# A bidirectional scan whose query-key products are kept for the other direction, with query norms taken from transposed tiles

## The chip, the cores and the metric

The kernel runs on one core of a Trainium2 chip. The metric is the device time of one execution in microseconds; smaller is better. Five engines work side by side and are tied by semaphores: TensorE (PE: matrix products and transposes into PSUM), VectorE (DVE), ScalarE (ACT), GpSimd (POOL) and SyncE (SP, which here only issues transfers). An engine works through its own instructions strictly in order, so an instruction that waits holds all those behind it.

## What is computed

One layer of a hybrid trunk on 1152 tokens (1024 latent ones and 128 context ones) of width 1024: a modulated norm, an input projection, a gated convolution group beside a bidirectional gated delta rule of 4 heads of width 128, an output projection, then a convolutional gated feed-forward part. The change is inside the delta rule only. Cut to what matters:

```python
def chunked_gated_delta(q, k, v, beta, log_alpha, s0):
    ...
    qk = jnp.einsum('bhnid,bhnjd->bhnij', q, k) * dec_incl
    ...
    def step(s, inp):
        u_c, w_c, qk_c, qd_c, ke_c, dl_c = inp
        v_new = u_c - jnp.einsum('bhcd,bhde->bhce', w_c, s)
        o_c = jnp.einsum('bhcd,bhde->bhce', qd_c, s) + jnp.einsum('bhij,bhje->bhie', qk_c, v_new)
        s = s * dl_c + jnp.einsum('bhcd,bhce->bhde', ke_c, v_new)
        return s, o_c
...
q = l2norm(q.reshape(b, l, DN_HEADS, DK)) * (DK ** -0.5)
...
o_f, s_f = chunked_gated_delta(q, k, v, beta[:, :, 0], log_alpha[:, :, 0], s0_f)
o_b, s_b = chunked_gated_delta(rev(q), rev(k), rev(v), ...)
o = o_f + rev(o_b)
```

The product of queries and keys of one tile of tokens is the same for both directions. Only the decay `dec_incl`, by which it is multiplied, differs.

## The kernel before, in words

The program first runs the input projection block by block, with the convolutions, the tables of decays and the inverses of the small triangular systems beside it. Then comes the scan, and then the output projection and the feed-forward part, where TensorE does products without a break.

The scan works on tiles of 128 tokens. `tile_of(d, x)` says which tile direction d (0 forward, 1 backward) treats at step x. Tiles 0 to 7 are the latent ones, and direction 1 takes them as 7, 6, ..., 0; step 8 is the context tile, number 8, for both. So each latent tile is treated twice: in steps 0 to 3 by one direction and in steps 4 to 7 by the other. Each engine has a hand-written order (`delta_pe`, `delta_act`, `delta_dve`, `delta_pool`), a loop over x from -1 to 8 that finishes step x (the scan part) and prepares step y = x + 1.

One round of TensorE, in order: `with_state(0)` (keys times state, then decayed queries times state), `first_products`, `with_state(1)`, `solve` for both directions, `closing` (from x = 6 on: transposes of finished outputs), `to_state(0)`, `second_products`, `queries(0)` (keys times queries of tile y), `to_state(1)`, `queries(1)`, `third_products`, `within(0)`, `query_rows`, `within(1)`, `fourth_products`. Each of the groups at line 1111 is four 128x128 products, one for each head. The first, second, third and fourth products build the inverse for the next tile from its blocks, with copies in between: M (DVE, L952), off-diagonal blocks (ACT, L736 and L740, in `off_blocks`, which also waits until DVE has written TX at L970, `low_diagonal`), LZ (DVE, L1025, `z_copy`) and the corner (ACT, L749). "First" to "fourth" below mean these products.

One round of VectorE: the wanted values (L908, `wanted`) of direction 0, M, the wanted values of direction 1, the diagonal (L960), `finish` (L941, from x = 6 on), `low_diagonal` (L970), new state 0 (L919), `values` (L979, twice), `weights(0)` (L985: keys-queries product from PSUM times decay R in SBUF), new state 1, `weights(1)`, `z_copy`, `second_out(0)` (L927, from x = 4 on), the copy of the query norms (L1030), `second_out(1)`, and from x = 5 on the sums of squares (L933, L935). POOL adds the mask to the decays R (L679, `masked`: both inputs in SBUF, when the transfer of the raw row has landed and `weights` has used the old R) and makes the decayed queries (L685, `decayed`, after an exponential on ACT, L812).

The squared norm of each query takes three steps: ACT squares the query tile (L820), TensorE multiplies the squares by a column of ones (L1171, `query_rows`, four products with one moving column), and DVE copies the four columns (L1030) to `ssq`, which only the output norm reads.

## Time and profile before

| | before |
|---|---|
| time, median of 3 runs | 1594.95 us (1590.67 to 1599.37) |
| the profiled execution | 1592.07 us, of which the span 1590.3 us |
| PE busy / DVE busy / ACT busy / POOL busy | 1530.6 / 942.6 / 476.4 / 398.4 us |
| chain that ended last | PE 86%, DVE 6%, DMA 3%, ACT 2%, issue 2% |
| the line with the scan's products (L1111) in that chain | 5% |
| TensorE clock granted over the span | 0.992 |

The median and the profiled execution are different executions of the same kernel. In the trace, times are counted from the start of the span. The scan lies between 466 and 621 us. A TensorE row "x8" of four products has eight records, since each of these float32 products is executed as two.

### The profile page before, as it was taken

The page shows a single profiled execution, that of the slowest core. Times are in us where ns is not written, and L with a number is a line of the kernel's source. Part 1 is how long each engine was busy: PE and PEld are TensorE (multiplying, and loading weights), DVE is VectorE, ACT ScalarE, POOL GpSimd, SP SyncE. Part 2 cuts the span into 40 slices and gives each one's busy share as a digit, 9 for nine tenths or more (in the row PEclk, how much of TensorE's full clock was granted, in tenths as well). Part 3 has the DMA queues.
Part 4 walks back from the last instruction along what each step waited for, and adds up shares of the span by engine and source line. Part 5 has one row for each costly group of instructions (what it writes and reads, how often), then busy time and mean ns, then how long its engine had stood idle before and what let it go on. Part 6 is the DMA issues. An engine that isn't in the chain of part 4 may idle for free.

```text
span 1590.3 us, 24156 instructions
## 1 busy us (share of the span) xinstructions
PE 1530.6 (96%) x9852; PEld 1474.9 (93%) x9852; DVE 942.6 (59%) x1407; ACT 476.4 (30%) x833; POOL 398.4 (25%) x204
## 2 busy tenths in 40 slices
PE   5899999999999998999999999999999999999997
PEld 1798999999989997998999999999999999999996
DVE  2752453569997795336885266528643673467257
ACT  4331254221166665125321032121212210221024
POOL 0011111560134343130231123113212321223120
PEclk9899999999999999999999999999999999999999
DMA  9543224532427446120111111111111111111103
GB/s 350 201 184 146 100 74 127 170 113 87 141 80 248 145 152 239 40 67 1 40 54 41 40 41 41 53 42 40 40 40 41 46 48 40 41 40 40 41 1 119
DMA packets 74641, 142.88 MB, mean 90 GB/s; under 512 B 19228, under 2 KB 44900, under 8 KB 72868
## 3 DMA queue, kind: packets, MB, share of 16 engines
q1 hardware_dynamic: 70932, 134.00, 25.0%
q10 hardware_dynamic: 3168, 5.51, 0.9%
q8 instruction: 87, 1.43, 0.4%
q0 software_dynamic: 432, 1.77, 0.3%
q14 instruction: 22, 0.18, 0.0%
HBM read 120.60 MB, written 20.65 MB: 89 GB/s over the span
## 4 chain that ended last, share of the span: by engine, by line
PE 86%; DVE 6%; DMA 3%; ACT 2%; issue 2%; SPq 1%; POOL 0%; DVEq 0%; ACTq 0%; POOLq 0%
PE ps L2312 49%; PE ps L2314 24%; PE ps L1111 5%; DMA araw<-wts 2%; PE ps L2253 1%; DVE ptmp L1922 1%; DVE lanes L1926 1%; PE ps L2263 1%; PE ps L2517 1%; DVE fa L2147 1%; PE ps L1084 1%; PE ps L2421 1%; DMA q<-q_d 0%; PE ps L2380 0%; PE ps L1056 0%
## 5 line engine op out<-in xcount | busy, mean ns | idle before, releaser
L2312 PE MATMUL ps<-hH,wH 128*128 128x384 f32 x1680 | 567.7, 338 | 7.3 <-DVE hL L1751 3.6
L2314 PE MATMUL ps<-hL,wH 128*128 128x384 f32 x1680 | 563.0, 335 | 0.0
L1225 POOL TENSOR_TENSOR wL<-raw,wH 128x1024 fp32r<-128x1024 f32 x93 | 226.2, 2432 | 887.3 <-ACT wH L1423 886.8
L2312 PE MATMUL ps<-hH,wL 128*128 128x384 f32 x1680 | 382.4, 335 | 0.0
L2312 PEld LDWEIGHTS ps<-hH,wH 128*128 128x128 f32 x1680 | 316.6, 188 | 15.2 <-issue 12.6
L1423 ACT ACTIVATE wH<-raw 128x1024 fp32r<-128x1024 f32 x99 | 105.1, 1062 | 710.4 <-PE ps L2312 709.4
L2314 PEld LDWEIGHTS ps<-hL,wH 128*128 128x128 f32 x1680 | 316.7, 189 | 0.0
L2147 DVE SCALAR_TENSOR_TENSOR fa<-G,cst,fa 128x1024 f32<-128x1024 f32 x176 | 295.5, 1679 | 15.4 <-DVE fa L2147 0.6
L2312 PEld LDWEIGHTS ps<-hH,wL 128*128 128x128 f32 x1680 | 300.2, 188 | 0.0
L2312 PE MATMUL ps<-pH,wH 128*128 128x384 f32 x528 | 179.2, 339 | 4.1 <-DVE pL L2171 1.8
L2034 DVE SCALAR_TENSOR_TENSOR X<-ps,mod,X 128x384 f32<-128x384 f32 x138 | 70.5, 567 | 188.9 <-PE ps L2312 188.9
L2314 PE MATMUL ps<-pL,wH 128*128 128x384 f32 x528 | 177.1, 335 | 0.0
L2312 PE MATMUL ps<-pH,wL 128*128 128x384 f32 x528 | 123.1, 336 | 0.0
L2143 DVE TENSOR_SCALAR fa<-G,cst 128x1024 f32<-128x1024 f32 x22 | 16.6, 753 | 164.3 <-ACT G L1439 164.3
L2312 PEld LDWEIGHTS ps<-pH,wH 128*128 128x128 f32 x528 | 99.7, 189 | 7.0 <-DVE X L2036 3.2
L2314 PEld LDWEIGHTS ps<-pL,wH 128*128 128x128 f32 x528 | 99.6, 189 | 0.7
L2312 PEld LDWEIGHTS ps<-pH,wL 128*128 128x128 f32 x528 | 94.8, 189 | 0.0
L1783 DVE TENSOR_SCALAR acc<-zp,wqk 128x1024 f32<-128x1024 f32 (+1 forms) x24 | 21.8, 946 | 72.7 <-ACT zp L1439 72.7
L1284 POOL TENSOR_TENSOR pL<-fa,pH 128x1152 fp32r<-128x1152 f32 x16 | 53.8, 3366 | 23.6 <-ACT pH L1645 23.6
L2253 PE MATMUL ps<-araw,scT 128*32 128x512 f32 x192 | 37.6, 686 | 18.5 <-DMA araw<-wts 18.3
L2253 PEld LDWEIGHTS ps<-araw,scT 128*32 128x32 f32 x192 | 6.2, 115 | 41.7 <-DMA araw<-wts 29.6
L2164 DVE TENSOR_TENSOR fa<-fa,ps 128x384 f32<-128x384 f32 x66 | 32.6, 548 | 11.8 <-PE ps L2312 11.8
(316 smaller groups left out, 1869.0 us busy)
## 6 DMA issues: line engine op xcount, KB each, us to landing
raw<-wts SPq DMA_DIRECT2D x103, 512.0 KB, 3.3
araw<-wts SPq DMA_DIRECT2D x48, 512.0 KB, 6.1
X<-xT SPq DMA_DIRECT2D x8, 1152.0 KB, 13.7
kv<-tok_d SPq DMA_DIRECT2D x16, 512.0 KB, 4.9
tok_d<-stage ACTq DMA_DIRECT2D x18, 256.0 KB, 2.0
q<-q_d SPq DMA_DIRECT2D x18, 256.0 KB, 5.8
gb<-grow_d SPq DMA_DIRECT2D x18, 256.0 KB, 3.6
y<-X SPq DMA_DIRECT2D x8, 384.0 KB, 2.4
```

Of the source, the lines that this page charges most:

```text
L1111: last = M(ps[:, k, h * P:h * P + P], left(h), right(h), start=(start if start is not None else h == 0), stop=(stop if stop is not None el ...
L1225: nc.gpsimd.tensor_tensor(weight(1, u4), raw[:, u4 % RAW, :], weight(0, u4).bitcast(F32), ALU.subtract).then_inc(s["wl_ready"], 1)
L1284: nc.gpsimd.tensor_tensor(pL[:, slot, :], fa[:, f % 2, :], pH[:, slot, :].bitcast(F32), ALU.subtract).then_inc(s["pL_ready"], 1)
L1423: A(weight(0, u4), raw[:, u4 % RAW, :], ACT.Copy).then_inc(s["wh_ready"], 1)
L1783: last = V.tensor_scalar(dst, src, w(tap), None, ALU.mult)
L2034: last = V.scalar_tensor_tensor(xs(lo, hi), bank3(side, n)[:, 0:hi - lo], mod[:, gate * 8 + ob, 0:1], xs(lo, hi), ALU.mult, ALU.add)
L2143: V.tensor_scalar(dst, src, w(3 * dy + dx), None, ALU.mult)
L2147: last = V.scalar_tensor_tensor(dst, src, w(3 * dy + dx), dst, ALU.mult, ALU.add)
L2164: last = V.tensor_tensor(fa[:, f4 % 2, n * TW:n * TW + TW], fa[:, f4 % 2, n * TW:n * TW + TW], bank3(side, n), ALU.mult)
L2253: last = M(ps[o:o + Q, ada_bank(m), :], scT[:, kt, :], araw[:, a % ARAW, 512 * j:512 * j + 512], start=(kt < 2), stop=(kt >= KT - 2))
L2312: last = M(out, lhs, rh[:, c], start=(k == 0 and not lo), stop=(lo and k == kts - 1))
L2314: M(out, lhs, rl[:, c], start=False, stop=False)
```

## The change

- `queries` (keys times queries) is done for steps 0 to 3 in both directions, and once in step 8. ACT copies each of the eight products of steps 0 to 3 from PSUM to SBUF tiles `KQ` (`keep`), after `weights` has used it. In steps 4 to 7 `weights` multiplies the kept tile instead of one in PSUM, so that both its inputs are in SBUF.
- In step 8 both directions use one product, and it is computed after the third products.
- Query norms: TensorE transposes the query tile (`query_rows`), ACT squares the transposed tile out of PSUM, and DVE sums the squares along each row (`query_sums`, 128x512 to 128x4). Those of step 0 are made in the round x = 0, after `with_state(0, 0)` and the first products.
- `low_diagonal` now stands ahead of `finish` on DVE.
- The loads of `ycA` (two of 1152 KB), whose place the kept tiles take until then, go from round y = 1 to y = 7 and y = 8; the load of the query tile of direction 0 waits for the transposes in place of the squares.

```diff
+    KQ = [place(f"KQ{k}", [P, H, P], F32, blk(14 - k // 4 * 2) + k % 4 * H * P * 4) for k in range(8)]
...
+    HALF = LAST // 2
+    def kept(d, y):
+        return KQ[2 * (LAST - 1 - y if y >= HALF else y) + (1 - d if y >= HALF else d)]
...
                     b, t = dl[d], tile_of(d, y)
-                    seen(sp, "qk", d, y)
+                    seen(sp, "qk", d, min(y, HALF))
                     seen(sp, "q_decayed", d, y)
                     if d == 0:
-                        sp.wait_ge(s["q_sq"], y)
+                        sp.wait_ge(s["trq"], y)
...
         def query_squares(act, y):
-            landed_at(act, "q_in", 0, y + 1)
+            act.wait_ge(s["trq"], y + 1)
             if y:
-                act.wait_ge(s["trq"], y)
+                act.wait_ge(s["q_sum"], y)
+            else:
                 act.wait_ge(s["solved"], 3)
-            nc.scalar.activation(qsq_of(y), q_of(0, y)[:], ACT.Square).then_inc(s["q_sq"], 1)
+            nc.scalar.activation(qsq, heads(bank_of(0)[3]), ACT.Square).then_inc(s["q_sq"], 1)
...
+            def keep(d, y):
+                seen(act, "pt", d, y + 1)
+                A(kept(d, y)[:], heads(bank_of(d)[3]), ACT.Copy).then_inc(s["kept"], 1)
...
                         new_values(d, x)
+                if x == 0:
+                    query_squares(act, 0)
...
+                if y < HALF:
+                    keep(0, y)
+                if 0 <= x < LAST // 2:
+                    first_out(0, x)
                 if 0 < y < TT_:
                     query_squares(act, y)
-                if 0 <= x < LAST // 2:
-                    first_out(0, x)
+                if y < HALF:
+                    keep(1, y)
...
             def weights(d, y):
                 b = dl[d]
-                seen(dve, "qk", d, y + 1)
                 seen(dve, "r_exp", d, y + 1)
-                done(V.tensor_tensor(b["PT"][y % 2][:], heads(bank_of(d)[3]), R_of(d, y), ALU.mult), "pt")
+                if y < HALF:
+                    seen(dve, "qk", d, y + 1)
+                    src = heads(bank_of(d)[3])
+                elif y < LAST:
+                    dve.wait_ge(s["kept"], 2 * HALF)
+                    src = kept(d, y)[:]
+                else:
+                    dve.wait_ge(s["qk"], 2 * HALF + 1)
+                    src = heads(bank_of(0)[3])
+                done(V.tensor_tensor(b["PT"][y % 2][:], src, R_of(d, y), ALU.mult), "pt")
+            def query_sums(y):
+                dve.wait_ge(s["q_sq"], y + 1)
+                V.tensor_reduce(ssq[:, tile_of(0, y), :], qsq, mybir.AxisListType.X, ALU.add).then_inc(s["q_sum"], 1)
...
+                if pre and y:
+                    low_diagonal(y)
                 for d, t, i in closed(x):
                     finish(d, t, i, bank_of(d)[3])
-                if pre and y:
-                    low_diagonal(y)
+                if x == 0:
+                    query_sums(0)
...
             def query_rows(y):
-                seen(pe, "pt", 0, y + 1)
-                pe.wait_ge(s["q_sq"], y + 1)
-                for h in range(H):
-                    last = M(ps[:, bank_of(0)[3], h:h + 1], qsq_of(y)[:, h, :], mat("ones")[:, 0:1], start=True, stop=True)
-                last.then_inc(s["trq"], 1)
+                seen(pe, "pt", 0 if y < LAST else 1, y + 1)
+                if y < HALF:
+                    pe.wait_ge(s["kept"], 2 * y + 1)
+                if y >= HALF:
+                    pe.wait_ge(s["q_sq"], y)
+                    seen(pe, "o_final", 0, max(y - 6, 0))
+                    landed_at(pe, "q_in", 0, y + 1)
+                turn(bank_of(0)[3], lambda h: q_of(0, y)[:, h, :]).then_inc(s["trq"], 1)
...
                 if x == 0:
+                    query_rows(0)
...
-                if pre:
+                if y < HALF:
                     queries(0, x, y)
                 if scan:
                     to_state(1, x)
-                if pre:
+                if y < HALF:
                     queries(1, x, y)
                 if pre and y:
                     third_products(pe, y)
+                if y == LAST:
+                    queries(0, x, y)
                 if scan:
                     within(0, x)
-                if pre:
+                if pre and y:
                     query_rows(y)
```

## Rows read from the trace of the kernel before

**Rows 1.** Busy by stretch: length, each engine, PE clock, DMA share, GB/s.

```profile
548.40:564.90 16.50, 16.50 (x219) 15.75 (x217) 13.85 (x32) 9.81 (x30) 7.76 (x7) 1.00 0.45 137
564.90:584.70 19.80, 19.80 (x248) 19.05 (x248) 18.58 (x36) 13.76 (x38) 13.14 (x10) 1.00 0.39 118
```

**Rows 2.** Chain that ended last, late in round x = 4: start, us, what.

```profile
548.42 2.88 PE ps L1111 x24
551.29 1.07 PE ps L1084 x16
...
553.46 0.79 PE ps L1171 x8
...
598.45 0.88 PE ps L1106 x8
```

**Rows 3.** Timeline of DVE, round x = 4: start, us, line, operation, [idle before].

```profile
543.78 1.13 DVE L908 SCALAR_TENSOR_TENSOR Y<-ps,SC,vb 128x128 f32<-128x128 f32 x4 [0.24 <-PE ps L1111]
...
551.37 0.68 DVE L985 TENSOR_TENSOR PTb<-ps,R 128x512 f32<-128x512 f32 x1
...
553.00 0.68 DVE L985 TENSOR_TENSOR PTb<-ps,R 128x512 f32<-128x512 f32 x1
553.60 0.73 DVE L1025 TENSOR_SCALAR LZ<-ps 64x256 f32<-64x256 f32 x2
...
557.26 1.13 DVE L908 SCALAR_TENSOR_TENSOR Y<-ps,SC,vb 128x128 f32<-128x128 f32 x4 [1.29 <-PE ps L1111]
```

**Rows 4.** Timeline of PE, same round and the next: fourth products' end, next round.

```profile
555.17 0.50 PE L1096 MATMUL ps<-LZ,TX 64*64 64x64 f32 x5
556.06 1.16 PE L1111 MATMUL ps<-S,QKV 128*128 128x128 f32 x8
```

**Rows 5.** Timeline of ACT, round x = 4.

```profile
550.42 0.27 ACT L740 ACTIVATE TX<-ps 32x128 f32<-32x128 f32 x1
...
551.90 0.61 ACT L820 ACTIVATE ptmp<-q 128x512 f32<-128x512 f32 x1
```

**Rows 6.** Timeline of POOL and DVE, round x = 4: where the two overlap.

```profile
549.06 1.84 POOL L685 TENSOR_TENSOR qd<-gb,q 128x512 f32<-128x512 f32 x1
549.68 1.76 DVE L979 TENSOR_TENSOR vb<-kv,SC 128x512 f32<-128x512 f32 x1
552.68 1.28 POOL L679 TENSOR_TENSOR R<-gb,cst 128x512 f32<-128x512 f32 x1 [1.78 <-DMA gb<-grow_d]
```

**Rows 7.** Lines: durations min/median/max of one, first and last start.

```profile
L979 DVE TENSOR_TENSOR vb<-kv,SC x16: 678/686/1777, 482.2 to 603.3; 128x512 f32<-128x512 f32 x16
```

**Rows 8.** Timeline of DVE and POOL, end of scan: a sum beside POOL's work.

```profile
616.20 0.69 DVE L933 TENSOR_REDUCE red<-osq 128x4 f32<-128x512 f32 x1 [5.56 <-POOL osq L693]
616.12 1.04 POOL L693 TENSOR_TENSOR osq<-oTok 128x512 f32<-128x512 f32 x1
```

**Rows 9.** Timelines of PE, ACT and POOL, start of the scan.

```profile
470.75 1.05 PE L1171 MATMUL ps<-cst,qd 128*128 128x1 f32 x8 [2.53 <-DVE PT L985]
471.60 1.04 ACT L1423 ACTIVATE wH<-raw 128x1024 fp32r<-128x1024 f32 x1
476.80 1.28 POOL L679 TENSOR_TENSOR R<-gb,cst 128x512 f32<-128x512 f32 x1 [0.72 <-DMA gb<-grow_d]
479.29 1.05 ACT L853 ACTIVATE Y<-ps 128x512 f32<-128x512 f32 x2
```

**Rows 10.** Timelines of DVE, PE and ACT, rounds x = 6 and 7.

```profile
583.63 1.46 DVE L970 TENSOR_TENSOR TX<-XT,cst 64x256 f32<-64x256 f32 x1
586.78 0.67 PE L1084 MATMUL ps<-TT,LZ 64*64 64x64 f32 x8 [1.70 <-ACT TX L740]
593.12 1.13 DVE L908 SCALAR_TENSOR_TENSOR Y<-ps,SC,vb 128x128 f32<-128x128 f32 x4
604.30 0.67 PE L1084 MATMUL ps<-TT,LZ 64*64 64x64 f32 x8 [1.10 <-ACT TX L740]
608.96 0.78 ACT L749 ACTIVATE TT<-ps 64x256 f32<-64x256 f32 x2 [2.89 <-PE ps L1096]
```

More of the change, by code:

```diff
@@ L637, in _ @@
                         og_load(d, tile_of(d, 4), 0)
[L638 to L639 removed]
+                if y in (HALF + 3, HALF + 4):
+                    k = y - HALF - 3
+                    seen(sp, "pt", 1, (HALF + 2, LAST)[k])
+                    sp.dma_start(ycA[:, 2 * k:2 * k + 2, :].bitcast(F32), yc_d[:, 4 * k:4 * k + 2, :].bitcast(F32)).then_inc(s["ycA_in"], 16)
             after_split(ahead - 1, U_OUT + 1 + RAW, 0)
```

24 lines of the change are left out of this document (10 added, 14 removed).

## Prediction

> **What bounds the kernel now.** I read in this order: the busy share by stretch, the chain that ended last, then each engine's timeline of one round. Outside the scan nothing changes, so only the stretch 466 to 621 us counts. By stretch, a middle round is 16.50 us long and PE is busy in all of it, DVE in 13.85 us; the round x = 6 with its neighbourhood shows DVE at 18.58 of 19.80 us [rows 1]. The chain says the same: in round x = 4 it stays on PE, three groups of four 128x128 products in 2.88 us, then the third products, then `query_rows` in 0.79 us [rows 2]. So a reader would take 0.96 us off for each group removed. But a busy PE only says that PE is the last of several engines that are nearly level. How far behind the others are is what their timelines show.
>
> DVE works from the wanted values of direction 1 at 543.78 without a gap to LZ, ending at 554.33 [rows 3]. The fourth products, which need LZ, start on PE at 555.17, and the next round at 556.06 [rows 4]. So PE can come forward by at most 0.77 us (keeping the 0.07 us that a handover takes) before it waits for DVE. On ACT the last off-diagonal block ends at 550.69 [rows 5], and the third products, which need it, start at 551.29 in the chain [rows 2]: 0.5 us of room. ACT and DVE both hang on products early in the same round, not on the ones removed. TensorE's clock is granted in full in these rounds (1.00) [rows 1], so it can gain nothing there.
>
> **The change part by part.** The sum is made against the profiled execution, 1592.07 us (span 1590.3); the median of the runs, 1594.95, is 2.9 above it, and I add that at the end.
>
> *Products dropped.* Eight groups in steps 4 to 7 and one in step 8, 9 x 0.96 = 8.6 us of PE [rows 2]. In rounds x = 3 to 5 PE then reaches the third products at 549.4 in place of 551.3 on the clock of round 4, and stands until ACT is done at 550.7. From there the order is third, `within(0)`, `query_rows`, `within(1)`, and then it waits for LZ. Of 1.9 us a round, 0.5 goes to the wait for ACT, or 0.77 at most comes through by DVE's limit.
>
> *The product from SBUF.* `weights` reads kept tile and decay, both in SBUF. A DVE operation of 128x512 with two SBUF inputs takes 686 ns undisturbed and 1777 when POOL is in its way [rows 7]; from PSUM the product took 680 [rows 3]. What the second figure is: `values` starts at 549.68 while POOL multiplies queries (549.06 to 550.90), and ends at 551.44, 0.54 behind POOL's end [rows 6]. `weights(0)` at 551.37 finds POOL idle. `weights(1)` at 553.00 falls into POOL's `masked(0)`, 552.68 to 553.96 [rows 3, 6]. Held in the same way it ends at 553.96 + 0.54 = 554.50 in place of 553.68: +0.82 us. LZ then ends at 555.15; the fourth products of direction 0 can start behind its first half and those of direction 1 behind its second, and the next round starts near 555.72 in place of 556.06. So -0.34 us a round, not -0.77. The bounds are the two: -0.77 (never held) and +0.9 (PE fully behind a product that waits for a whole mask). I take -0.34, by the row it repeats. The Trainium skill ("SBUF — State Buffer", section "Who interferes with whom") has the rule: a VectorE instruction with two SBUF inputs and a GpSimd instruction that reads SBUF exclude each other for the whole instruction, and one with a single SBUF input is free. By that rule, the product held before was free and is not now; the trace agrees in the 1777 ns row. The skill's "VectorE: DVE Perf Modes", in its section on the TRN2 errata, speaks for the change: a fixed 58 cycles with an SBUF source against 120 from PSUM, an estimate of 65 ns a product and 0.5 us for eight; the trace (686 against 680 ns) doesn't show it, and the sum leaves it out.
>
> *Query norms.* Transposes of a tile took 0.88 us (L1106) against 0.79 for the products with one column [rows 2]: +0.09 in each of the nine rounds; on the path only in x = 0 to 2, +0.27, since in the others PE waits anyway. ACT squares as before, 0.61 us [rows 5], but later, between `query_rows` and the corner, where it has room. DVE's copy of four columns becomes a sum over 128x512, 0.69 us, not held by POOL (it ran beside POOL's square) [rows 8]: +0.54 a round, behind LZ. Its cover is DVE's gap before the next wanted values, 1.29 us in round 4 [rows 3]. From x = 5 on the sums of squares fill that gap: at 593.12 the wanted values start with no idle time before them [rows 10]. There it counts.
>
> *Copies kept.* Eight on ACT, 0.6 us each (its copies and squares of 128x512) [rows 5], in rounds x = -1 to 2. The first of a round starts when `weights(0)` ends, 0.6 us before `query_rows` needs it. Behind them on ACT stand the square, the corner and the exponentials of the next round, and ACT is busy in 9.81 of the 16.50 us of a round [rows 1]: 0, and if that cover is gone 0.6 each.
>
> *Start.* PE had waited 2.53 us for the first product before `query_rows(0)` [rows 9]; with the state products ahead of it that wait is filled. But behind the move `with_state(1)` waits for the first copy, and ACT makes it after the weights' half at 471.60 to 472.64, so near 473.3; transposes to 474.2; and the next stage waits anyway: ACT's new values at 479.29 come behind exponentials that wait for POOL's mask at 476.80, which waits for a transfer [rows 9]. 0, with -0.3 and +0.5 as bounds (SP's query load, now behind the transposes, had been issued about when they end).
>
> *Loads moved.* SP's queue: `ycA`, in round y = 1, competed for transfers; in y = 8 it stands ahead of the gate tiles of the next `finish` and ahead of `ycB`, needed after 621 us; in the round of x = 6 the transfer engines are busy for 0.39 of the time [rows 1]. 0; 1 at the bound if that cover is gone.
>
> *Late rounds.* x = 5: DVE's end of round comes 0.54 + 0.78 later, and its gaps before the next M and wanted values take that up, so nothing of PE's gain is left: 0. x = 6: `low_diagonal` ahead of `finish` releases ACT's blocks, for which PE stood 1.70 us [rows 10], but at that place it meets POOL's squares and then its query products; I take 0.6 us earlier (bounds 0 and 1.9). Then sum, held product and `finish`, now behind it, put the next wanted values +0.65. x = 7: the last product stands behind the third products. From their start to the fourth it was 3.9 us; now it is third 1.07, product 0.96, the two `weights` from it 1.35, transposes 0.9, `within(1)` 1.0 = 5.3, and the third start 0.2 later than at 604.30. So the corner on ACT, 608.96 before [rows 10], comes +1.45 us later (including x = 6), and table loads, norms and the last step all hang on it.
>
> Sum: start 0, x = 0 to 2 +0.27, x = 3 and 4 2 x -0.34 = -0.68, x = 5 0, x = 6 and 7 +1.45: **+1.0 us**, 1593.1 on the profiled execution, 1596.0 on the median. 8.6 us of TensorE work go into waits.
>
> **Rivals.** (a) *PE's time comes through in full*: -8.6 + 0.8 for transposes = -7.8, 1584.3 own, 1587.2 median. For it: PE is busy in every row. Against: DVE's unbroken chain to LZ. (b) *The product is not held, and `low_diagonal` gets its turn*: -0.77 in x = 3 and 4, about 1 us less in x = 6 and 7: -1.0, 1591.1 own, 1594.0 median. (c) *Slower: both products are held.* If POOL's second query product ends more than 0.47 us later than 550.90, it covers the start of `weights(0)` too, and masks follow; each of rounds 3 to 6 then costs a further mask, 1.27 us: +1.0 + 5.1 = 1598.2 own, 1601.1 median. (d) *The copies on ACT reach the path* in x = -1 to 2 (they do not hide): 8 x 0.6 = +4.8, 1597.9 own, 1600.8 median.
>
> **How the numbers follow.** Forecast 0.70, (b) 0.13, (a) 0.04, (c) 0.08, (d) 0.05. The time is the forecast's, 1596.0. The three runs of before spread by 4.4 us to either side of their median, and the median of the changed kernel will miss its own level by some 2 or 3; forecast and (b) with that reach from 1589 to 1600, and 1601 takes in part of (c) and (d). Within 0.5% (8 us, about what a measurement here can tell from no change) lie all cases, (a) only just: faster 0.03, same 0.94, slower 0.03.
>
> **What would show it.** Rounds x = 3 to 5 of about 16.2 us with PE idle before the third products (waiting for ACT's TX) and before the fourth (waiting for DVE's LZ); PE busy some 8 us less in a scan of the same length; one of two `weights` a round near 1.5 us beside `masked`; `low_diagonal` in x = 6 ending near 584.5; the corner of x = 7 later against its round. Wrong if rounds x = 3 to 5 are near 14.6 us (then LZ doesn't bound), if the held product stays at 0.69, or if rounds 0 to 2 grow by over 0.3 us.

## The result, and the profile after

The changed kernel takes 1610.38 us (median of 4 runs, 1609.22 to 1612.67) beside 1594.49 for the kernel before in the same comparison (4 runs, 1590.67 to 1599.37). The ratio is 1.010 with a 95% interval of 1.0069 to 1.013: slower by 1%. I had forecast 1596.0 and a range of 1589 to 1601. In the later comparisons, of 24 to 28 runs each, the median of the kernel before is 1596.8 to 1598.9 us with single runs from 1588.8 to 1604.4; every ratio below is to the kernel before in the same comparison, and every trace is one execution.

| | before | after |
|---|---|---|
| the profiled execution / its span | 1592.07 / 1590.3 us | 1609.58 / 1607.8 us |
| first query-key product starts | 466.3 | 465.2 |
| from there to the next stage's first product (the scan) | 155.0 | 161.1 |
| of it, up to the first product of round x = 1 (the start) | 23.8 | 26.8 |
| of it, each of the rounds x = 1, 2 / 3 / 4, 5 | 16.49 / 16.50 / 16.49 | 16.04 / 15.95 / 17.12 |
| of it, rounds x = 6 / 7 with the last step | 19.06 / 29.61 | 19.27 / 32.76 |
| from there to the end | 969.0 | 981.5 |
| TensorE clock granted over the span | 0.992 | 0.982 |

So the 17.5 us between the two profiled executions are +6.1 in the scan, -1.1 ahead of it, and +12.5 behind it, where the change touches no computation. But the +6.1 is the difference of two single executions. The traces of pad24, pad224, bpad32 and bmatch (below) hold the same two scans once more each, as they only have more wait instructions at the start of the program (us):

| trace | start | x = 1, 2 | x = 3 to 5 | x = 6, 7 | scan |
|---|---|---|---|---|---|
| code of before: before | 23.8 | 33.0 | 49.5 | 48.7 | 155.0 |
| bpad32 | 24.6 | 33.0 | 49.5 | 53.4 | 160.4 |
| bmatch | 24.6 | 33.0 | 49.5 | 53.3 | 160.3 |
| changed code: after | 26.8 | 32.1 | 50.2 | 52.0 | 161.1 |
| pad24 | 23.3 | 32.1 | 50.4 | 52.0 | 157.8 |
| pad224 | 23.1 | 32.1 | 52.0 | 53.0 | 160.1 |

What repeats is -0.9 us in x = 1 and 2 and +0.7 to +2.5 in x = 3 to 5. The start and the two late rounds differ as much between traces of one code as between the codes. By the means, 158.6 and 159.7, the scan is 1 us longer, and the loss is what lies behind it.

Lines of the changed kernel: L1143 is the helper that was L1111, L1116 the third products, L1138 the transposes, L1011 `weights`, L997 `values`, L746 ACT's TX, L2351 and L2353 the later stages' products.

The busy share by stretch of the changed kernel, rounds x = 4, 5, 6 and x = 7 with the last step:

```profile
core 0: us, PE busy (x) PEld busy (x) DVE busy (x) ACT busy (x) POOL busy (x), PEclk, DMA share, GB/s
539.99:557.11 17.12, 15.90 (x198) 15.03 (x197) 14.84 (x31) 9.82 (x30) 6.68 (x6) 0.90 0.50 157
557.11:574.23 17.12, 15.89 (x199) 15.03 (x197) 14.88 (x32) 9.87 (x30) 7.26 (x6) 0.90 0.44 131
574.23:593.50 19.27, 16.71 (x207) 15.50 (x205) 18.66 (x37) 13.12 (x36) 10.94 (x8) 0.91 0.59 193
593.50:626.26 32.76, 24.53 (x254) 22.79 (x253) 22.57 (x43) 21.58 (x51) 12.02 (x11) 0.90 0.74 258
```

Against [rows 1], 20 records of PE are gone in a round and the round is longer, because PEclk is 0.90 where it was 1.00: in 0.2 of each round TensorE ran at 1.2 GHz in place of 2.4. The timeline of PE in round x = 4 shows where:

```profile
548.77 1.16 PE L1143 MATMUL ps<-Y,ke 128*128 128x128 f32 x8
551.15 0.71 PE L1116 MATMUL ps<-TT,LZ 64*64 64x64 f32 x8 [1.22 <-ACT TX L746]
551.66 1.06 PE L1116 MATMUL ps<-TX,LZ 64*64 64x64 f32 x8
552.65 2.07 PE L1143 MATMUL ps<-Y,PT 128*128 128x128 f32 x8
554.52 0.87 PE L1138 MATMUL ps<-cst,q 128*128 128x128 f32 x4
```

PE stands 1.22 us for ACT's TX, as the prediction said it would, and then a group of four products takes 2.07 us in place of 1.16. DVE in the same round:

```profile
551.75 0.68 DVE L1011 TENSOR_TENSOR PTb<-KQ,R 128x512 f32<-128x512 f32 x1
553.38 1.44 DVE L1011 TENSOR_TENSOR PTb<-KQ,R 128x512 f32<-128x512 f32 x1
554.75 0.74 DVE L1058 TENSOR_SCALAR LZ<-ps 64x256 f32<-64x256 f32 x2
```

One of the two `weights` is held to 1.44 us where it was 0.68 [rows 3]. Behind the scan, the timeline of PE at the head of the feed-forward loop, and the row of the waits view for 626 to 1607 us (in total, times, longest):

```profile
919.52 0.44 PE L2351 MATMUL ps<-hH,wH 128*128 128x384 f32 x1 [0.91 <-issue]
...
920.15 0.33 PE L2353 MATMUL ps<-hL,wH 128*128 128x384 f32 x1
922.57 0.33 PE L2351 MATMUL ps<-hH,wH 128*128 128x384 f32 x1 [2.08 <-issue]
```

```profile
PE ps L2351 <- issue: 10.6, 8, 2.1
```

At each of the four passes from the loop's end back to its head PE stands 1.8 to 2.1 us, a few products behind the head, and 0.5 to 0.9 us just ahead of them, and waits for nothing that the profile shows. Before, the same four places have one gap of 0.44 to 0.50 us:

```profile
1065.21 0.44 PE L2312 MATMUL ps<-hH,wH 128*128 128x384 f32 x1 [0.44 <-issue]
```

### The profile page after: what moved, and what is told of

It is laid out like the page before. It is cut to its first block, busy times and chain, and to the rows that moved or that the text cites. A ratio compares the mean times of both kernels' runs of the same rounds, so it can differ in the third digit from the quotient of the medians.

```text
span 1607.8 us, 23941 instructions
## 1 busy us (share of the span) xinstructions
PE 1534.0 (95%) x9744; PEld 1477.2 (92%) x9744; DVE 949.7 (59%) x1407; ACT 480.2 (30%) x841; POOL 403.7 (25%) x204
## 4 chain that ended last, share of the span: by engine, by line
PE 88%; DVE 5%; ACT 3%; DMA 2%; issue 2%; POOL 0%; DVEq 0%; ACTq 0%; SPq 0%; POOLq 0%
PE ps L2351 51%; PE ps L2353 25%; PE ps L1143 4%; DMA araw<-wts 2%; PE ps L2292 2%; DVE TT L978 1%; PE ps L2302 1%; PE ps L2556 1%; PE ps L1116 1%; DVE fa L2186 1%; PE ps L1088 1%; PE ps L2460 0%; PE ps L2419 0%; PE ps L1138 0%; DVE X L2073 0%
## 5 line engine op out<-in xcount | busy, mean ns | idle before, releaser
L2351 PE MATMUL ps<-hH,wH 128*128 128x384 f32 x1680 | 569.7, 339 | 16.1 <-issue 10.6
L2353 PE MATMUL ps<-hL,wH 128*128 128x384 f32 x1680 | 564.8, 336 | 0.0
L2351 PE MATMUL ps<-hH,wL 128*128 128x384 f32 x1680 | 384.3, 336 | 0.0
L2351 PEld LDWEIGHTS ps<-hH,wH 128*128 128x128 f32 x1680 | 318.0, 189 | 16.1 <-issue 13.3
L2353 PEld LDWEIGHTS ps<-hL,wH 128*128 128x128 f32 x1680 | 318.2, 189 | 8.7 <-issue 8.7
L2186 DVE SCALAR_TENSOR_TENSOR fa<-G,cst,fa 128x1024 f32<-128x1024 f32 x176 | 300.9, 1710 | 15.4 <-DVE fa L2183 0.6
L2351 PEld LDWEIGHTS ps<-hH,wL 128*128 128x128 f32 x1680 | 301.8, 189 | 0.0
L2351 PE MATMUL ps<-pH,wH 128*128 128x384 f32 x528 | 179.4, 340 | 4.0 <-DVE pL L2210 1.8
L2353 PE MATMUL ps<-pL,wH 128*128 128x384 f32 x528 | 177.2, 336 | 0.0
L2351 PE MATMUL ps<-pH,wL 128*128 128x384 f32 x528 | 122.9, 335 | 0.0
L2351 PEld LDWEIGHTS ps<-pH,wH 128*128 128x128 f32 x528 | 99.6, 189 | 7.0 <-DVE X L2075 3.2
L2353 PEld LDWEIGHTS ps<-pL,wH 128*128 128x128 f32 x528 | 99.7, 189 | 0.7
L2351 PEld LDWEIGHTS ps<-pH,wL 128*128 128x128 f32 x528 | 94.8, 189 | 0.0
L1325 POOL TENSOR_TENSOR pL<-fa,pH 128x1152 fp32r<-128x1152 f32 x16 | 58.4, 3648 | 8.6 <-ACT pH L1684 8.6
```

The source lines that it names most:

```text
L1325: nc.gpsimd.tensor_tensor(pL[:, slot, :], fa[:, f % 2, :], pH[:, slot, :].bitcast(F32), ALU.subtract).then_inc(s["pL_ready"], 1)
L2186: last = V.scalar_tensor_tensor(dst, src, w(3 * dy + dx), dst, ALU.mult, ALU.add)
L2351: last = M(out, lhs, rh[:, c], start=(k == 0 and not lo), stop=(lo and k == kts - 1))
L2353: M(out, lhs, rl[:, c], start=False, stop=False)
```

## The experiments

The theory after the first look had two parts. L (loop): the change took 224 instructions out of PE's stream ahead of the feed-forward loop (by my count of the program), and the place of the loop's head in the stream decides what the jump costs. C (clock): with the products gone PE waits once more in a round, and TensorE's clock falls. The rival of L is that something else behind the scan changed (transfers, buffers); the rival of C is that the waits or the held product alone lengthen the rounds.

**pad24, pad224 and bpad32: the place of the loop's head.** All stand at the head of PE's program. Twice as many waits as instructions are written, as two go into one: 49 in pad24, 449 in pad224, and in the kernel before 65 for bpad32.

```diff
-            pe.wait_ge(s["sc_ready"], 2)
+            for _ in range(49):
+                pe.wait_ge(s["sc_ready"], 2)
```

> The changed kernel with 24 more instructions in TensorE's stream ahead of its first product (48 waits on a semaphore that already has its value, two to an instruction); nothing else. In the changed kernel TensorE stands about 2.1 us eleven instructions behind the head of its feed-forward loop, in four of five passes, with no engine that it waits for. Theory L (where the loop's head lies in the instruction stream decides whether the fetch behind the jump is late, and the change moved it by some 220 instructions): the head moves past that place, the four stalls go, and with them the half-clock stretches behind them at 922 and 1075 us: 8 us from the stalls and 2 to 5 us from the clock, so 1598 to 1601 us. Rival D (the stall comes from data, memory traffic or the engines beside it): 1610, stalls as before.

Measured: 1594.77 us (1591.35 to 1595.89; ratio to before 0.9978, interval 0.9959 to 0.9996). No gap at the loop's head; 966.5 us behind the scan (981.5), and the rounds x = 1 to 5 as in the changed kernel. 24 instructions more, 15.6 us less, and below the 1598 to 1601 that I expected. The half-clock stretch at 780 us, behind a wait for ACT, is there as in the changed kernel (at 782.5), so it is not the loop's.

> The changed kernel with 224 instructions more ahead of TensorE's first product, which puts the head of the feed-forward loop back to where it is in the kernel before (the change took 216 product and load instructions and 8 waits out). Theory L: no stall behind the loop's head, 1598 to 1601 us, the same as with 24. Rival D: 1610. If the scan alone made the whole loss, both stay at 1610.

Measured: 1609.54 us, ratio 1.007 (1.0049 to 1.0091): the expected time was missed, the mechanism not. The loop's gaps are 0.43 to 0.98 us and the part behind the scan takes 968.3 us as before. But PE's first product starts at 28.5 us in place of 5.1: the 224 waits themselves cost 0.10 us each, and the first query-key product comes 14 us late.

> The kernel before with 32 instructions more ahead of TensorE's first product. If the fetch works in blocks of 64, 128 or 256 instructions, the loop's head then lies against the blocks as in the changed kernel (224 less is 32 more). Theory L: the kernel before gets the four stalls of 2.1 us and some clock behind them, 1602 to 1607 us. Rival D: 1594, no stalls.

Measured: 1610.98 us, ratio 1.0085 (1.0058 to 1.0112), above the 1602 to 1607 expected. The kernel before, its computation unaltered, is as slow as the changed one, and shows the same gaps:

```profile
1075.89 0.44 PE L2313 MATMUL ps<-hH,wH 128*128 128x384 f32 x1 [0.96 <-issue]
...
1078.92 0.34 PE L2313 MATMUL ps<-hH,wH 128*128 128x384 f32 x1 [2.06 <-issue]
```

That excludes the rival of L: nothing that the change does to transfers or buffers is in this kernel.

The passes also show how gaps and clock share the loss. One pass, from a row that stands in each to its next, for example

```profile
868.43 0.44 PE L2351 MATMUL ps<-pH,wH 128*128 128x384 f32 x1 [0.32 <-DVE X L2075]
```

```profile
1023.79 0.45 PE L2351 MATMUL ps<-pH,wH 128*128 128x384 f32 x1 [0.32 <-DVE X L2075]
```

| | four passes, us | half the clock for 3.4 us in |
|---|---|---|
| before | 151.15, 151.07, 151.10, 151.11 | none |
| after | 155.36, 154.86, 153.19, 153.47 | the first (923.7) and second (1077.3) |
| bpad32 | 155.40, 153.81, 153.69, 153.66 | the first (923.7) |
| pad24 | 150.36, 150.36, 150.35, 150.36 | none |

The four passes hold 12.45 us of the +12.5. A pass with the gaps alone takes 153.2 to 153.8 us, one with a half-clock stretch behind them 1.1 to 2.2 us more.

**fill: an unused product in PE's wait.** In x = 3 to 5, four products of 128x128 (keys by the identity) into bank 3 of direction 1, which nobody reads then.

```diff
+                if HALF <= y < LAST - 1:
+                    idle_products()
                 if pre and y:
                     third_products(pe, y)
```

> The changed kernel with four products of 128x128 whose result nobody reads, in rounds x = 3, 4 and 5, where TensorE waits for the off-diagonal blocks; they go to PSUM bank 3, which is idle there (48 instructions more, so the loop's head moves too). In the changed kernel rounds 4 and 5 take 17.1 us, with the clock at half for 3.4 us in each. Theory C (the idle time ahead of the third products lets the clock fall, and that makes these rounds longer than before): the clock stays at 1.00 in rounds 3 to 5 and they take 15.9 to 16.1 us, 2.2 us less in the scan. Rival W (the waits for ScalarE and VectorE alone make them long, the clock is no matter): 17.1 us with the filler too. By theory L the feed-forward stalls are gone as well: in all 1595 to 1599 us; by D and C 1608.

Measured: 1589.26 us, ratio 0.9964 (0.9939 to 0.9989), below the 1595 to 1599 expected, with rounds of 16.2 to 16.3 us where I had expected 15.9 to 16.1. Round x = 5 by stretch, and PE in round x = 4:

```profile
552.43:568.66 16.23, 15.33 (x207) 14.44 (x205) 15.08 (x32) 9.88 (x30) 7.70 (x7) 1.00 0.47 140
```

```profile
547.25 0.68 PE L1116 MATMUL ps<-TT,LZ 64*64 64x64 f32 x8 [0.33 <-ACT TX L746]
...
549.32 0.60 PE L1138 MATMUL ps<-cst,q 128*128 128x128 f32 x4
...
551.50 0.50 PE L1128 MATMUL ps<-LZ,TX 64*64 64x64 f32 x5 [0.69 <-DVE LZ L1058]
```

Work that nobody uses makes the round 0.8 us shorter than with an idle PE. This isn't one trace's luck. after, pad24, pad224 and free0, with PE idle there, all fall to half the clock in x = 4 and 5 (17.1 to 18.7 us a round), and late3, free3, best3, own, own7 and own8, with the unused product, never do in x = 3 to 5 (15.5 to 16.1). And now the wait for LZ that I had forecast shows, 0.69 us: with the clock at half PE had been too late to meet it.

**free3 and free0: the held product, with and without the unused products.**

```diff
         def masked(pool, d, y):
-            seen(pool, "pt", d, y)
+            for k in range(2):
+                seen(pool, "pt", k, y)
```

> The kernel with unused products in rounds x = 3 to 5 (fill), and besides both of POOL's masks of a round wait until both weights products of DVE are done, so that weights(1), now with two SBUF inputs, cannot be held by masked(0). Nothing is left out. Theory 'weights(1) is held by the mask and its 0.7 us bounds the round' (the prediction's term +0.82 minus 0.77): weights(1) takes 0.69 us instead of 1.4, LZ and the fourth products come 0.7 us sooner, rounds x = 3 to 5 take 15.6 us instead of 16.28, the masks start 0.7 us later at no cost; time 2 us under fill. Rival 'the masks are wanted as soon': exponentials on ACT wait for them, the next round's new values slip by what was won, rounds stay at 16.3 and the time is that of fill.

Measured: 1589.35 us, ratio 0.9964 (0.9943 to 0.9986). The rounds went as expected, the time did not: x = 3, 4, 5 take 15.55, 15.54, 15.54 us, and the second `weights` in the round x = 4, which ends at 556.07, is

```profile
553.92 0.68 DVE L1012 TENSOR_TENSOR PTb<-KQ,R 128x512 f32<-128x512 f32 x1
```

The 2.2 us less in these three rounds don't show in the medians (1589.26 and 1589.35), whose single runs spread by 5 us and more. In free0 the masks are as in free3, without the unused products and with 48 wait instructions' worth at the start, so that the loop's head stands where it does in fill.

> The changed kernel with POOL's masks behind both weights products, without unused products; 48 waits' instructions in PE's waits of the first 25 us, so its loop head stands where that of fill and free3 does. Nothing is left out. With the changed kernel (hold, no filler: rounds x = 4, 5 of 17.12 us), fill (hold, filler: 16.3) and free3 (no hold, filler: 15.54) it completes the square. Theory 'hold and clock are two causes that add': weights(1) in 0.69 us, PE stands 1.2 us ahead of the third products, the clock falls to half for 3.4 us a round in x = 3 to 5 or 4 and 5, these rounds take 16.3 us; time 2 us above free3. Rival 'without the hold PE stands only once a round and keeps its clock': rounds of 15.2 to 15.5, time at or under free3's 1589.

Measured: 1593.3 us, ratio 0.9973 (0.9955 to 0.999). The square of the two causes, from seven traces (rounds x = 3, 4, 5 in us):

| | PE idle in the wait | unused product in it |
|---|---|---|
| `weights(1)` held | after 15.95, 17.12, 17.12; pad24 16.16, 17.10, 17.10; pad224 16.20, 18.63, 17.13 | fill 16.27, 16.34, 16.22; late3 15.95, 15.98, 16.08 |
| not held | free0 15.55, 17.11, 18.65 | free3 15.55, 15.54, 15.54 |

```profile
540.07:557.19 17.12, 15.89 (x199) 15.02 (x197) 14.20 (x31) 9.87 (x30) 7.25 (x6) 0.90 0.53 163
557.19:575.84 18.65, 17.44 (x198) 16.47 (x197) 15.27 (x33) 9.85 (x30) 7.35 (x6) 0.82 0.49 148
```

I had expected 16.3 us for the two causes apart. They are two causes, but they don't add: with the clock at half, taking the hold away brings nothing in x = 4 and 5, since PE is then the last again.

**norms3 and norms48: the change's one half alone.** The kernel before, with the norms of tiles 1 to 8 from transposed tiles, and every product computed twice. norms48 has 145 more wait instructions in PE's waits of the first 50 us.

```diff
-                for h in range(H):
-                    last = M(ps[:, bank_of(0)[3], h:h + 1], qsq_of(y)[:, h, :], mat("ones")[:, 0:1], ...)
+                turn(bank_of(0)[3], lambda h: q_of(0, y)[:, h, :]).then_inc(s["trq"], 1)    # y > 0
```

> The kernel before with one half of the change: for tiles y = 1 to 8 the query norms come from transposed tiles squared on ACT and summed on DVE; tile 0 as before, all query-key products computed twice as before, low_diagonal and the loads as before. Its loop head lies 65 instructions before that of the kernel before, 159 behind that of the changed kernel, so by the position theory no 2-us stalls. Theory by the records of the changed kernel (a tile's transposes are 4 records in 0.6 us, not 8 in 0.88 as I had read): PE is on the path of rounds x = 1 to 5 and each takes 16.0 to 16.1 us instead of 16.5, without a wait of PE over 0.5 us and with the clock granted in full; late rounds +0.5 each for the sums; the scan 1 to 2 us shorter than before and the time about 1594 beside a before of 1596. Rival 'as I had priced it': rounds 16.6, scan 1 us longer, 1598.

Measured: 1594.58 us, ratio 0.9979 (0.9964 to 0.9995). Rounds x = 2 to 5 of 16.03 or 16.04 us with PE busy in all of it:

```profile
537.36:553.40 16.04, 16.04 (x215) 15.29 (x213) 13.76 (x31) 9.87 (x30) 5.50 (x5) 1.00 0.47 142
```

> The kernel norms3 (only the norms changed, every product computed twice) with 145 more wait instructions on PE in its waits of the first 50 us, so that its loop head stands where that of bmatch does, 304 behind the changed kernel's (48 past a multiple of 256). Nothing is left out. Theory 'position': no gaps at the loop's head (0.44 to 0.86 us in norms3), 965.5 us from the next stage's first product to the end (970.0 in norms3, 965.9 in bmatch), rounds x = 1 to 5 of 16.03 to 16.05 us with the clock in full, as in norms3; time 3 to 4 us under norms3's 1594.6 unless the added waits reach past PE's own waits (then the first query-key product comes later than 470 and the gain is eaten up). Rival 'norms3 was slow after the scan for another reason': 970 us again.

Measured: 1592.68 us, ratio 0.996 (0.9946 to 0.9975). No gaps at the head, 966.0 us behind the scan (970.0 in norms3). Beside bmatch (below), whose head stands at the same place and whose ratio is 1.0007, this half of the change makes the kernel faster, by some 0.4%.

**bmatch: the kernel before with its head at the good place.** 80 more wait instructions, in three of PE's own waits in the first 25 us.

> The kernel before with 80 more wait instructions on PE in its waits of the first 25 us (about 80 ns each, in gaps of 2.1, 2.1 and 5.2 us), so that its loop head stands 304 instructions behind that of the changed kernel, which is 48 behind a place where it stalls if the pattern repeats every 256 instructions, the place of fill. Nothing is left out. In the kernel before, 224 behind, PE stands 0.44 to 0.5 us at four of five passes of the loop, and from the next stage's first product to the end it takes 969.1 us; in fill, late3 and free3 (48 behind) no such gap and 964.5 to 966.1 us. Theory 'position, with a period of 256 instructions': no gaps over 0.4 us at the loop's head, 965 us from that product to the end, the scan as before (131 us from x = 1), time 3 to 5 us under the kernel before of the same runs. Rival 'the gaps and the 4 us come from the kernels' other parts': gaps of 0.44 us, 969 us, same time as the kernel before.

Measured: 1596.69 us, ratio 1.0007 (0.9991 to 1.0022). No gaps, 966.0 us behind the scan: the place is confirmed. The time is not: it is that of before, where I had expected 3 to 5 us less, and why is open. Its profiled execution shows a scan of 160.3 us with code that took 155.0 in the profile of before; 3.2 of the 5.4 us are in round x = 6, 1.5 in x = 7:

```profile
572.18:594.42 22.24, 20.54 (x226) 19.57 (x225) 18.99 (x40) 13.24 (x36) 10.72 (x8) 0.84 0.49 153
```

bpad32 has the same round (22.15 us). So the clock falls in x = 6 of the kernel before too, in two of three executions, behind the same wait of 1.70 us [rows 10], and the rows of before happened to show one where it didn't.

The place of the head over all traces, as instructions behind that of the changed kernel:

| head | kernels | gaps at the four passes, us | behind the scan, us |
|---|---|---|---|
| 0, 256 | after, bpad32 | 1.83 to 2.36 each, and 0.54 to 1.00 ahead of it | 981.5, 981.0 |
| 24, 48 | pad24, fill, late3, free3, free0, own, own7, own8 | none over 0.4 | 964.5 to 966.5 |
| 304 | bmatch, norms48 | none over 0.4 | 966.0, 966.0 |
| 72, 113, 120, 159, 224 | kept, best3, keptfill, norms3, before, pad224 | up to 0.4 to 1.0 | 968.3 to 970.1 |

It repeats with 256 instructions (0 with 256, 48 with 304); the differences of 1.5 us within the second row go with half-clock stretches of 3.4 us, which fill and free3 (964.5) lack at the start of this part. The Trainium skill ("Runtime: NRT & Kernel Launch", section "Instruction fetch mechanics") states that instructions come in blocks of 256 and that a taken branch breaks the sequential prefetch; the period in the traces agrees, with 1.8 to 2.4 us a jump at the worst place. That PE waits for a fetch there no row shows; the rows say only that it waits for nothing else.

**kept and keptfill: the other half.** kept is the changed kernel with the norms of the kernel before; keptfill adds the unused products of fill. Its start is not that of the changed kernel: the first `query_rows` is at its old place and must now wait for a copy on ACT (below).

> The other half of the change alone: query-key products kept for the other direction and not computed twice, low_diagonal ahead of finish and the loads as in the changed kernel, but the query norms as in the kernel before (squares of the queries on ACT, four products with one column, DVE's copy of four columns; tile 0 at its old place). Loop head 72 instructions behind that of the changed kernel, so no 2-us stalls. Nothing is left out. Theory 'the dropped products are what costs': rounds x = 1, 2 of 16.5 us as before, PE stands about 1 us ahead of the third products in x = 3 to 5, the clock falls to half there, these rounds take 17.1 us (16.5 before); from the first query-key product to the next stage 158 us (155.0 before, 154.9 with the norms alone); time 1 to 2 us above the kernel before less what the position gives back, 1595. Rival 'the norms' sums behind LZ are what costs': rounds x = 3 to 5 of 16.2 us, scan as short as before or shorter, 1590.

Measured: 1611.17 us, ratio 1.0098 (1.0061 to 1.0134), with no 2-us gaps at the loop. Right in kind for the clock, far off in size (1595 expected): it was at half for 17.1, 10.2 and 13.7 us, from 555.5, 579.4 and 599.9 (the expectations of this part give such times some 2 us too early). Rounds x = 4, 5, 6:

```profile
544.00:563.71 19.71, 18.49 (x203) 17.47 (x201) 14.45 (x31) 9.98 (x30) 7.41 (x7) 0.79 0.56 171
563.71:586.74 23.03, 21.82 (x202) 20.71 (x201) 15.70 (x34) 9.78 (x29) 5.88 (x5) 0.65 0.33 100
586.74:608.75 22.01, 20.96 (x210) 19.94 (x209) 17.59 (x39) 13.14 (x35) 10.36 (x8) 0.73 0.46 150
```

> The kernel kept (products kept for the other direction, old norms) with four unused products ahead of the third products in x = 3 to 5, as in fill. In kept TensorE had half its clock for 17.1, 10.2 and 13.7 us from 553, 577 and 598, and rounds x = 3 to 5 took 19.7, 23.0 and 22.0 us; the time was 1611.2. Loop head 48 instructions behind that of kept, gaps of 0.5 to 1 us there as in kept. Nothing is left out. Theory 'the dropped products cost through the clock alone': no half-clock stretch in x = 3 to 5, these rounds take 16.3 to 16.6 us, from the first query-key product to the next stage 157 us (174.9 in kept), time about 1595. Rival 'the kept half costs by its waits or copies': the rounds stay above 18 us and the time above 1605.

(The expectation's "x = 3 to 5" for these three rounds is off by one: they are x = 4 to 6.) Measured: 1603.26 us, ratio 1.0024 (1.0006 to 1.0041), 8 us less by adding work:

```profile
546.98:563.10 16.12, 15.77 (x211) 14.88 (x209) 13.84 (x31) 9.80 (x30) 5.17 (x5) 1.00 0.46 141
563.10:579.09 15.99, 15.66 (x210) 14.84 (x208) 14.32 (x33) 9.74 (x30) 7.41 (x7) 1.00 0.46 139
579.09:600.91 21.82, 19.58 (x211) 18.55 (x209) 19.89 (x41) 13.24 (x36) 11.89 (x9) 0.80 0.65 215
```

Where the unused products stand (x = 4, 5) the clock is full and 10.6 us are gone; x = 6, without them, is as long as in kept. The scan is 11 us shorter (163.9 for 174.9) but not the 157 expected, and both theories hold in part. The start took 29.0 us in kept and 28.6 in keptfill (23.8 before), since the first `query_rows` stood for the copy of the first product, which ACT makes only behind its work on the next stage's weights (471.37 to 472.41):

```profile
472.31 1.05 ACT L863 ACTIVATE KQ<-ps 128x512 f32<-128x512 f32 x2
```

```profile
472.98 1.84 PE L1209 MATMUL ps<-cst,qd 128*128 128x1 f32 x8 [5.03 <-issue]
```

So in the rounds this half costs through the clock, and at the start through a copy: the prediction's rival (d), in a place that the whole change avoids.

**late3, best3, own, own7, own8: the late rounds.** late3 is fill with the last product ahead of the third products; best3 adds unused products in x = 0, 6 and 7; own is free3 with the last product ahead of the third and `finish` ahead of `low_diagonal` for the last tile; own7 fills x = 7 by a bank that doesn't wait for `finish`; own8 besides moves a load:

```diff
-                if y in (HALF + 3, HALF + 4):
-                    k = y - HALF - 3
...
-            after_split(ahead - 1, U_OUT + 1 + RAW, 0)
+                if y == HALF + 3:
+                    ycA_load(0)
             for d in range(2):
                 og_load(d, tile_of(d, 5), 1)
+            ycA_load(1)
+            after_split(ahead - 1, U_OUT + 1 + RAW, 0)
```

> The kernel with unused products in rounds x = 3 to 5 (fill), and besides the last query-key product (x = 7) ahead of the third products instead of behind them. Nothing is left out; one product group changes its place, no instruction is added. In fill PE stood 3.37 us ahead of the third products of x = 7 (till 600.17), the product ran 602.04 to 604.1 at half the clock, DVE stood 3.29 us for it, and the corner on ACT started 607.75, 20.3 us behind the round's first product (17.3 in the kernel before). Theory 'the late round is long because the last product stands behind the third products' (the prediction's step): the product runs near 599.1 when finish of direction 0 is done, inside the wait; the two weights follow values without a gap (near 600.9), the corner comes 2 to 3 us sooner against its round (17.3 to 18.3 us), next stage 31 us behind the round's start instead of 33.4, time about 1587. Rival 'DVE's and POOL's new order (low_diagonal held by POOL, finish behind it) makes the round long': corner at most 0.5 us sooner, time 1589.

Measured: 1589.85 us, ratio 0.995 (0.9931 to 0.9969), x = 7 to the next stage 32.88 us (33.46 in fill), which is within what this stretch spreads by between traces. The theory fell: the product still ran only at 602.42, behind a wait of 2.53 us for DVE's `finish`, and the third products behind it.

> The changed kernel with unused products in all long waits of PE in the scan: ahead of the third products in rounds x = 3 to 7 (16 instructions each), and two groups at x = 0 ahead of query_rows(0), where PE stood 2.2 us for the first copy; the last query-key product ahead of the third products as in late. Loop head 113 instructions behind the changed kernel's. Nothing is left out. Theory 'clock and last product together explain the scan': no half-clock stretch between 466 and 621, x = 7 to the next stage 30 us, the scan 5 us shorter than in fill, no loop stalls, time about 1584, 0.8% under the kernel before. Rival 'the waits of x = 0, 6 and 7 are not where the clock is lost, or the unused products lengthen the round': time that of late, 1587, or above.

Measured: 1596.31 us, ratio 0.9989 (0.997 to 1.0009). A miss: its clock still fell at 478.6 and 601.5, as the unused products of x = 6 and 7 themselves waited for `finish` (3.07 us in x = 7), and its head stood at 113.

> The changed kernel with three things together, nothing left out: unused products in the wait of rounds x = 3 to 5 (as fill), POOL's masks behind both weights products (as free3), and in the last tile's round (x = 7) the last query-key product ahead of the third products (as late3) with finish ahead of low_diagonal, in the order of the kernel before. Loop head 48 instructions behind the changed kernel's. In late3 the product still stood 2.53 us for finish, which stood behind low_diagonal (held by POOL's squares), and ran at 602.42. Theory 'the late round is long because the last product hangs on finish, which the change put behind low_diagonal': the product runs within 0.5 us of the end of DVE's finish and before ACT's TX, PE's third products follow TX at once, x = 7 to the next stage 30 us (33.5 in fill, 32.9 in late3, 29.6 in the kernel before), rounds x = 3 to 5 15.5 us, from the first query-key product to the next stage 150.5 us (before 155.0, free3 153.0), time about 1586. Rival 'TX then comes later by what finish takes (1.4 us)': x = 7 stays at 32 us or more and the time is that of free3, 1589.

Measured: 1591.58 us, ratio 0.9951 (0.9934 to 0.9968); x = 7 took 34.64 us, longer than in late3. The rows of DVE and SP say why:

```profile
600.72 1.57 DVE L960 SCALAR_TENSOR_TENSOR oTok<-ps,onw,og 128x512 f32<-128x512 f32 x2 [2.34 <-DMA og<-gd]
```

```profile
589.53 0.65 SPq L645 DMA_DIRECT2D ycA<-yc  x1
590.23 0.42 SPq L493 DMA_DIRECT2D raw<-wts  x1
590.70 12.14 SPq L608 DMA_DIRECT2D og<-gd  x4
```

> As own, but three unused products (12 instructions) in place of four in rounds x = 3 to 5, and three more in x = 7 ahead of the last query-key product, into a bank that is free there, so that they don't wait for finish. In own PE stood 2.38 and 1.32 us in x = 7, TensorE had half its clock for 10.2 us from 598.2, and x = 7 to the next stage took 34.6 us. Nothing is left out. Theory 'the clock is most of what x = 7 loses': half for 3.4 us or less there, x = 7 to the next stage 32 us; rounds x = 3 to 5 15.2 to 15.5 us; time 2 us under own's 1591.6. Rival 'the gate tiles' transfer is all of it': x = 7 stays at 34 us, time that of own.

Measured: 1588.46 us, ratio 0.9943 (0.9925 to 0.9961); x = 7 33.74 us with `finish` still waiting 1.46 us, half the clock for 6.8 us from 597.0. Between the two theories.

> As own7, and besides the second ycA load (and the weights' load behind it) stand behind the gate tiles of the next finish in SP's queue, not ahead of them. In own DVE's finish of x = 7 stood 2.34 us for the gate tiles (issued 590.7, landed near 600.7) behind ycA (issued 589.5, 1152 KB); in the kernel before ycA had been loaded in x = 0. Nothing is left out. Theory 'the moved load holds the gate tiles' (my bound of 1 us in the prediction): finish follows diagonal with no wait (near 598.4 on own's clock), product, TX, third products 2 us sooner, x = 7 to the next stage 30 us, the time 2 us under own7, near 1587. Rival 'the tiles land no sooner, the transfer engines being full': finish still waits over 1.5 us, time that of own7.

Measured: 1586.45 us (4 runs, 1582.83 to 1588.66), ratio 0.9915 (0.9882 to 0.9947). `finish` follows with no wait, half the clock for 3.4 us from 603.4, x = 7 in 31.50 us (x = 6 and 7 together 49.5, 52.5 in own7):

```profile
597.62 1.40 DVE L963 SCALAR_TENSOR_TENSOR oTok<-ps,onw,og 128x512 f32<-128x512 f32 x2
```

```profile
588.63 1.35 SPq L608 DMA_DIRECT2D og<-gd  x2
590.03 2.93 SPq L612 DMA_DIRECT2D ycA<-yc  x1
```

This version beats both kernels, by 0.85% (interval 0.5 to 1.2%) and, across comparisons, 1.5%. Most of the second figure is the place of the loop's head: pad24, which is the changed kernel with its head at a good place, took 1594.77 us, 0.5% more than own8.

## Why the prediction was wrong, and where it was right

**The step that failed worst: "Outside the scan nothing changes".** +12.5 of the +17.5 us lie there, by the place of the loop's head; pad24 takes 15.0 of the 981.5 us away, bpad32 puts 12 onto the kernel before. The gaps themselves are 8.8 us (10.6 against 1.8, in total), and most of the rest are the two half-clock stretches behind them, at 924 and 1077, by the lengths of the passes above. This step alone takes the time out of the range.

**The step that failed beside it: "TensorE's clock is granted in full in these rounds (1.00), so it can gain nothing there".** It can lose. I had put 8.6 us of PE's work into waits and priced the waits at nothing. With PE idle for 1.22 us ahead of the third products the clock fell in x = 4 and 5 (0.90), +0.63 us a round, where my sum had -0.34 and 0. fill, free3, kept and keptfill show it from both sides. Why x = 3, with the same wait, keeps its clock, and why kept loses it for so much longer than the whole change, no run tells apart.

**The scan as a whole, +1.0.** The means of three traces of either code give +1.1, but that would be luck: -0.9 in x = 1 and 2, where I had +0.2, and +1.4 in x = 3 to 5 on the mean, where I had -0.7, are two misses that cancel, and the spread of several us in the start and in x = 6 and 7 is larger than either.

**Transposes, +0.09 a round.** Mis-read: "x8" in 0.88 us [rows 2] was two tiles. One tile is 4 records in 0.60 us, and the next group starts 0.44 us behind them (fill, norms3), in place of 0.81 behind the products with one column. Rounds x = 1 and 2 are 0.45 us shorter, not 0.09 longer, as are x = 2 to 5 of norms3, so PE's path takes this through in full. The +0.27 of the start and two rounds should have been near -0.9.

**Held product, +0.82: right.** 1.44 us for 0.68 in x = 4 (1.22 to 1.61 in x = 3 to 5 of after and fill), and LZ 14.76 us behind the round's first product in place of 14.01. With the clock in full the round is 15.9 to 16.3 us (16.16 by my sum), and 15.54 without the hold.

**Waits for ACT and for LZ: right** in place (1.22 and, in fill, 0.69 us). **Copies, 0: right** for the whole change: x = 2 takes 16.03 us with them and 16.03 in norms3 without. At the start only the moved `query_rows(0)` keeps them off the path, as kept shows. **A sum of 0.54 more behind LZ: right** as far as x = 2 to 5 show, 16.03 us with it.

**Start, 0, at most +0.5: right on the mean, too narrow for one execution.** It was 26.8 us in the profiled execution, and 23.3 and 23.1 in pad24 and pad224 (23.8 to 24.6 before). In the long one POOL held both `values`, where fill, with the same code, had them half held and took 23.8:

```profile
482.89 4.34 DVE L997 TENSOR_TENSOR vb<-kv,SC 128x512 f32<-128x512 f32 x2
```

```profile
480.93 2.48 DVE L997 TENSOR_TENSOR vb<-kv,SC 128x512 f32<-128x512 f32 x2
```

So some 2 of the 3 us are a collision that comes and goes; the clock was low there too (0.79 from 466 to 490 us).

**Late rounds, +1.45.** Measured +3.4, but not shown: x = 6 and 7 of the kernel before take 48.7, 53.4 and 53.3 us in three traces, those of the changed one 52.0, 52.0 and 53.0. My terms for x = 7 also add to 1.4 + 0.2 = 1.6, not 1.45. The order was read rightly: DVE stood 2.9 us for the last product. Putting that right alone brought 0.6 us (late3), within the spread: behind it stood `finish`, and behind that the gate tiles. **Loads moved, 0 with 1 at the bound**: in the changed kernel nothing waited, since `finish` came later still; once it doesn't, it waits 2.34 us (own) or 1.46 (own7), and moving the load takes that wait away (own8); x = 7 was 2.2 us shorter there, of which the clock is a part and spread may be another.

My sum for the rounds x = 3 and 4, the heart of the argument, holds within 0.3 us in every kernel whose clock is full and whose product is held; for x = 5 the sum had 0 and the round came 0.3 to 0.6 us shorter. The forecast failed in what it had closed off ahead of the sum.

## What to carry to other kernels

Work that is taken from an engine ahead of a wait is no free gain on TensorE: price the idle time as clock too, and if the wait can't go, leave something in it. Any edit that changes the number of TensorE's instructions moves every loop behind it; look at the gaps at the loop's head before a change is blamed, and compare kernels with the head at the same place. Compare by rounds and stages of the trace, and look at the same round in several executions before a difference of a few us is given a cause: here +6.1 us between two traces shrank to +1.1 between the means of three.

## What the runs showed of the hardware

- A jump back to a loop's head cost TensorE from under 0.4 us to a gap of 1.8 to 2.4 us with another of 0.5 to 1.0 ahead of it, by the head's place in a pattern of 256 instructions; 24 more instructions were worth 15.0 us in four passes (981.5 and 966.5 us behind the scan).
- Groups of four products of 128x128 take 1.16 us at 2.4 GHz and 2.07 at 1.2. With one wait of 1.22 us in a round of 16 to 17 us the lower level appeared for 3.4 us in a round, and for up to 17.1 us at a stretch in kept; with four unused products in that wait (0.33 us left of it) it did not. The same scan kept its full clock in x = 6 in one trace and had half for 10.2 us in two others.
- Instructions that only wait cost 0.07 to 0.10 us each: 24, 32 and 224 of them moved PE's first product by 1.6, 3.0 and 23.4 us; without them it starts at 4.7 to 5.5 us.
- A VectorE product of 128x512 with two SBUF inputs took 1.44 us in the changed kernel, beside POOL's mask, and 0.68 with the mask moved behind it (free3).
